# Weight scales from sums of squares on ScalarE, and attention's probabilities turned in nine whole pieces

## What is computed

```
layer 0:  proj = rms_norm(x) @ w_in        -> u, z_a, h, b, c, z_b (512 columns each)
          y_a  = pool_mixer(u) * silu(z_a) # running means over windows 2, 4, 8, 16, less u,
                                           # a 128x128 map for each group, a scale
          y_b  = b * conv3(c * h) * silu(z_b)
          x    = x + concat(y_a, y_b) @ w_out
layer 1:  proj = rms_norm(x) @ w_in        -> query latent (768), key/value latent (256),
                                           # shared rotary key (32), gate (1024)
          q, k, v from the latents: 16 heads, 64 + 32 wide; rms_norm of q and k per head
          p    = softmax(mask(q @ k.T)); o = p @ v  # causal, in blocks of 128 queries
          x    = x + (o * silu(gate)) @ w_out
```

## Time and profile before

| | us |
|---|---|
| median of 3 runs (range) | 961.5 (960.9 to 961.76) |
| the profiled execution, span | 960.9 |
| PE busy | 947.5 (99%) |
| DVE busy | 812.9 (85%) |
| ACT busy | 575.2 (60%) |
| POOL busy | 353.1 (37%) |
| DVE line 2497 (`low`), 192 operations | 102.1, 554 ns each |
| ACT line 2360 (`high`), 192 operations | 89.1 |

### The profile page before, as it was taken

The page is one execution under the profiler, slowest core; times in us unless marked ns, Lnnn a source line. Parts: engine busy times, 40 slices in busy tenths (PEclk is TensorE's granted clock), DMA queues, the critical chain, the costliest instruction groups (busy, mean ns, idle before and its releaser), DMA issues.

```text
span 960.9 us, 17257 instructions
## 1 busy us (share of the span) xinstructions
PE 947.5 (99%) x6406; PEld 671.3 (70%) x6406; DVE 812.9 (85%) x1410; ACT 575.2 (60%) x1076; POOL 353.1 (37%) x393
## 2 busy tenths in 40 slices
PE   9999999999999999999999999998999999999998
PEld 8788544444688887644457999996788888887443
DVE  5798899899865579988887899998999999998763
ACT  6443544424434454454646888866899989997230
POOL 0002233222000002235412577875652478894220
PEclk9999999999999999999999999999999999999999
DMA  9320422111054422332123264566676775460231
GB/s 305 45 61 23 110 77 56 44 45 45 1 175 155 152 67 67 107 112 58 31 72 111 89 205 150 204 181 176 119 163 145 171 150 122 82 179 2 88 110 65
DMA packets 165347, 103.74 MB, mean 108 GB/s; under 512 B 75272, under 2 KB 149520, under 8 KB 165008
## 3 DMA queue, kind: packets, MB, share of 16 engines
q1 hardware_dynamic: 159216, 102.25, 38.0%
q10 hardware_dynamic: 6048, 0.39, 0.5%
HBM read 56.48 MB, written 29.36 MB: 89 GB/s over the span
## 4 chain that ended last, share of the span: by engine, by line
PE 72%; DVE 19%; POOL 3%; issue 3%; ACT 2%; DVEq 0%; POOLq 0%; ACTq 0%
PE banks L111 19%; PE banks L113 19%; PE banks L112 19%; PE banks L2728 7%; PE banks L2746 2%; PE banks L2748 2%; PE banks L2747 2%; DVE heads_y L2480 1%; POOL heads_prod L2616 1%; DVE heads_x L2476 1%; DVE heads_x L2475 1%; DVE front_lt L1223 1%; DVE heads_ss L2522 1%; PE banks L2756 1%; DVE front_l L1223 1%
## 5 line engine op out<-in xcount | busy, mean ns | idle before, releaser
L2497 DVE TENSOR_TENSOR heads_pt_lo<-banks,heads_pt_hi 128x512 f16<-128x512 f32 (+2 forms) x192 | 102.1, 554 | 10.8 <-ACT heads_pt_hi L2360 7.8
L2360 ACT ACTIVATE heads_pt_hi<-banks 128x512 f16<-128x512 f32 (+2 forms) x192 | 89.1, 487 | 9.1 <-PE banks L2728 8.9
L2748 PE MATMUL banks<-heads_v,heads_pt_lo 128*128 128x64 f16 x576 | 71.1, 194 | 0.0
L2747 PE MATMUL banks<-heads_v,heads_pt_hi 128*128 128x64 f16 x576 | 71.0, 194 | 0.0
L2489 DVE CUSTOM_DVE_ANT_0 heads_probs_big<-banks,heads_mask,score_scale 128x1024 f32<-128x1024 f32 (+1 forms) x64 | 68.6, 1072 | 2.9 <-PE banks L113 2.7
L2746 PE MATMUL banks<-heads_v,heads_pt_hi 128*128 128x64 f16 x576 | 70.9, 194 | 0.0
L2728 PE MATMUL banks<-ident,heads_probs_big 128*128 128x128 f32 x416 | 69.5, 281 | 1.2 <-ACT heads_probs_big L2351 1.1
L2351 ACT ACTIVATE heads_probs_big<-heads_probs_big,heads_neg_max 128x1024 f32<-128x1024 f32 (+1 forms) x64 | 63.4, 990 | 8.8 <-DVE heads_neg_max L2489 7.7
L111 PE MATMUL banks<-heads_k_t,heads_q_t 96*128 96x512 f16 (+2 forms) x192 | 63.0, 328 | 1.0 <-DVE heads_neg_max L2489 1.0
L111 PE MATMUL banks<-front_act_hi,front_w_hi 128*128 128x512 f32 x160 | 63.8, 399 | 0.0
L113 PE MATMUL banks<-front_act_hi,front_w_lo 128*128 128x512 f32 x160 | 62.4, 390 | 0.0
(11 more groups left out here) (489 smaller groups left out, 3114.5 us busy)
## 6 DMA issues: line engine op xcount, KB each, us to landing
qk_scratch<-heads_y SPq DMA_DIRECT2D x22, 512.0 KB, 3.7
front_x<-in_x_t SPq DMA_DIRECT2D x16, 512.0 KB, 5.3
front_raw<-in_w_in_ab SPq DMA_DIRECT2D x14, 512.0 KB, 5.1
qk_scratch<-heads_last_y SPq DMA_DIRECT2D x10, 512.0 KB, 3.8
front_w<-in_w_out_ab SPq DMA_DIRECT2D x8, 512.0 KB, 3.9
x_scratch<-front_x SPq DMA_DIRECT2D x8, 512.0 KB, 3.9
v_scratch<-heads_v SPq DMA_DIRECT2D x32, 128.0 KB, 3.0
heads_v_st<-v_scratch SPq DMA_DIRECT2D x8, 512.0 KB, 5.2
```

Of the source, the lines that this page charges most:

```text
L2360: nc.scalar.activation(pt_hi[:, q % PIECES, :width], t_ps[:, banks[("piece", n, k)] % 3, :width], ACT.Copy).then_inc(pt_high, 1)
L2497: nc.vector.tensor_tensor(pt_lo[:, q % PIECES, :width], t_ps[:, banks[("piece", n, k)] % 3, :width], pt_hi[:, q % PIECES, :width], ALU.sub ...
L2747: nc.tensor.matmul(o_part, pt_hi[:, q % PIECES, blk], v2[e][:, j, VH:], start=False, stop=False)
L2748: last = nc.tensor.matmul(o_part, pt_lo[:, q % PIECES, blk], v2[e][:, j, :VH], start=False, stop=(j == i))
```

## The change

1. `pair_peak` and `peak` go. ACT gets `pair_norm`: one ACTIVATE with Square over the same 128x2048 weights, whose accumulated sum per partition takes the place of the maximum. Its elementwise result goes to a scratch tile. It stands behind ACT's snapshot 1 and ahead of `first_tap` and snapshot 2 in pairs 1 to 6; behind snapshot 1 in pairs 8 to 12; other places for pairs 0, 1, 8 and the three of the output.
2. `norm_scale` takes the scale from the sum of squares: one more DVE operation than before.
3. `pair_scale` moves: in `conv` from before the wait for the tap to the end, in `pool_sums` from the middle to the end.
4. PE's `row_sum` moves behind i = 3 in pairs 1 to 12.
5. Attention: another `ORDER`, and nine pieces per head, each a whole 512 columns; three of the nine hold blocks of two tiles. The order of the turns and products within a step, and the access patterns of what comes behind, follow from it. The number of turned blocks and of products stays.

```diff
-ORDER = (7, 3, 6, 2, 5, 1, 4, 0)
+ORDER = (7, 3, 5, 1, 6, 0, 4, 2)
+PIECE_BLOCKS = ([(0, j) for j in range(4)], [(0, j) for j in range(4, 8)], [(1, j) for j in range(4)],
+                [(2, j) for j in range(4)], [(2, 4), (2, 5), (3, 0), (3, 1)],
+                [(4, j) for j in range(4)], [(4, 4), (4, 5), (4, 6), (5, 0)],
+                [(6, j) for j in range(4)], [(6, 4), (7, 0), (7, 1), (7, 2)])
...
+def norm_scale(nc, link, total, size, scale):
+
+    top = float(0x5F3759DF + (13 << 23))
+    link(nc.vector.tensor_scalar(size, total, TINY, None, ALU.max))
+    link(nc.vector.tensor_scalar(scale.bitcast(I32), size.bitcast(I32), -0.5, top, ALU.mult, ALU.add))
+    link(nc.vector.reciprocal(size, scale))
...
+        def pair_norm(p):
+            raw_landed(act, p)
+            if p > 1:
+                act.wait_ge(row_spread, p - 1)
...
+            source = x[:, 0:CHUNKS, BANK:] if p == 0 else raw(p)[:].rearrange("p m (h k) c -> p (m h) (k c)", h=2)
+            nc.scalar.activation(dump[:], source, ACT.Square, accum_out=w_row[:, p % 2:p % 2 + 1]).then_inc(row_peak, 1)
...
                 snapshot(p, 1)
+                if p and p + 1 < PAIRED:
+                    pair_norm(p + 1)
                 if p and p % 2 == 0:
                     first_tap(g - 1)
...
                 snapshot(p, 1)
+                if not last_pair:
+                    pair_norm(p + 1)
...
         high(ROPE0)
+        pair_norm(PAIRED)
         pair_forms(PAIRED, range(FORMS))
...
                 src, n, step = dst, n + 1, 2 * step
-            if p < PAIRED:
-                pair_scale(p)
             link(nc.vector.tensor_scalar(head[:, :win], count[:, :win], float(win), None, ALU.min))
...
             nc.vector.tensor_tensor(d_lo[:], other, f32(d_hi[:]), ALU.subtract).then_inc(d_ready, 1)
+            if p < PAIRED:
+                pair_scale(p)
...
             dve.sem_inc(ch_ready, 1)
-            if p < PAIRED:
-                pair_scale(p)
             dve.wait_ge(tapped, g + 1)
...
             link(nc.vector.tensor_tensor(acc, acc, bb[:], ALU.mult))
             dve.sem_inc(convolved, 1)
+            if p < PAIRED:
+                pair_scale(p)
...
-        def pair_peak(p):
-            raw_landed(dve, p)
-            if p > 1:
-                dve.wait_ge(row_spread, p - 1)
-            nc.vector.tensor_reduce(w_row[:, p % 2:p % 2 + 1], x[:, 0:CHUNKS, BANK:] if p == 0 else
-                                    raw(p)[:].rearrange("p m k c -> p (m k c)"), AX_XY if p == 0 else AX_X, ALU.max,
-                                    apply_absolute_value=True).then_inc(row_peak, 1)
...
-            link(nc.vector.tensor_scalar(w_size[:, one], spread_ps(p), TINY, 2.0 ** -13, ALU.max, ALU.mult))
-            link(nc.vector.reciprocal(w_scale[:, one], w_size[:, one]))
+            norm_scale(nc, link, spread_ps(p), w_size[:, one], w_scale[:, one])
...
                     pair_product(p, i)
-                    if p + 1 < PAIRED and i == (1 if p else 4):
+                    if p + 1 < PAIRED and i == (3 if p else 4):
                         row_sum(p + 1)
...
                     pair_product(p, i)
-                    if p + 1 < ALL_PAIRS and i == 2:
+                    if p + 1 < ALL_PAIRS and i == 3:
                         row_sum(p + 1)
...
+    def pieces_at(n):
 
         h, p = divmod(n, NT)
-        return PER_HEAD * h + sum(len(pieces(ORDER[x])) for x in range(p)) + k
+        return [PER_HEAD * h + x for x, blocks in enumerate(PIECE_BLOCKS) if blocks[-1][0] == p]
...
-            if k == 0:
-                pe.wait_ge(exp_done, n + 1)
-            for r, j in enumerate(pieces(tile_of(n)[1])[k]):
+            pe.wait_ge(exp_done, blocks_of(q)[-1][0] + 1)
+            for r, (n, j) in enumerate(blocks_of(q)):
...
-            for k in range(max(new_pieces, old_pieces)):
-                if k < new_pieces:
-                    transposes(n, k)
-                if k < old_pieces:
-                    product(old, k)
+            for k in range(max(len(new_pieces), len(old_pieces))):
+                if k < len(new_pieces):
+                    transposes(new_pieces[k])
+                if k < len(old_pieces):
+                    product(old_pieces[k])
```

More of the change, by code:

```diff
@@ L2414, in scalar @@
             if n < N:
-                for k in range(len(pieces(tile_of(n)[1]))):
-                    high(n, k)
+                for q in pieces_at(n):
+                    high(q)
             if n + AHEAD < N:
@@ L2437, in scalar @@
         for q in range(1, out.OUT_PAIRS):
+            out.pair_norm(act, q)
             out.forms_high(act, q)
@@ L2543, in vector @@
             if n < N:
-                for k in range(len(pieces(tile_of(n)[1]))):
-                    low(n, k)
+                for q in pieces_at(n):
+                    low(q)
                 if n % 4 == 3:
```

119 lines of the change are left out of this document (61 added, 58 removed).

## The result

The changed kernel takes 971.25 us (median of 4 runs, 970.54 to 972.53) against 961.63 for the kernel before: a ratio of 1.010, 95% interval 1.0087 to 1.0113, so 9.6 us slower. The forecast was 963.7 with a range up to 967.0. The side was right; the size was not.

A forecast was written before the change was run, and what follows sets the result against it. PE was taken as the bound, busy for 947.5 of 960.9 us. Norm and scale +6.6, pair 1 -0.9, pairs 3, 5, 7 +0.3, pairs 8 to 13 -1.4, attention -2.5: +2.1 on 961.5, rounded to 963.7; range 960.2 to 967.0.

The forecast's parts named there:

- norm ahead of the tap, pairs 2, 4, 6: ACT's norm, taken as 1.95 us, makes the tap 1.5, 1.1 and 1.35 us later: +3.95.
- bare scale, the same pairs: At the end of `conv` nothing hides the scale: 0.9 us per pair, +2.7, between 1.5 and 2.7.
- pair 1: `row_sum` moves behind product 3, past the wait for ACT's snapshot, and nothing replaces that wait: -0.88 us.
- pairs 3, 5, 7: Pair 3 stays free of a stall and pair 5 gets 0.3 us worse: +0.3, between -0.4 and +0.7.
- pair 8: DVE reaches the scale earlier, so the stalls of 0.53 and 0.74 us go: -1.27, between 0 and -1.27.
- pair 11 and the rest to 13: Pair 11 gains 0.35 of its 1.19 us; later row sums in pairs 12 and 13 cost +0.2.
- attention, all of it: Fewer switches and smaller stalls at its start and end: -2.5 us, from -0.5 to -4.5.
- switches saved: In attention, one turn per head instead of four stands right behind a product: -1.5 us.
- end: At attention's end, spread short tiles and joined pieces leave 0.1 of a 0.61 us stall: -0.5.
- rival 2: The clock falls behind the front's new waits, one to three stretches of 1.7 us: 965.4 to 968.8; chance 0.12.
- rival 5: POOL's sums block DVE's doublings in pairs 3 and 5, 1.6 us on top: 965.2; chance 0.08.
- signs of being wrong: Tap not late; three stalls growing under 3 or over 9 us; attention's 690 to 865 changing by over 4.5 us.

The follow-up runs named there:

- scales_only: Parts 1 to 4 of the change alone on the kernel before, with attention as before: 969.08 us, ratio 1.0077.
- reduction_back: The changed kernel with DVE's reduction over the weights put back in pairs 1 to 6 and 8 to 12, its result unused: 973.94 us, ratio 1.0126.

## Why the prediction was right or wrong

The number failed in attention above all, where -2.5 was forecast and +2.6 came. The terms, by the starts of PE's matmuls in the profiled executions:

| step | forecast | measured |
|---|---|---|
| norm ahead of the tap, pairs 2, 4, 6 | +3.95 | +3.7 |
| bare scale, the same pairs | +2.7 | +2.2 |
| clock behind those waits | a rival, 0.12 | +1.7 |
| pair 1 | -0.88 | +0.34 |
| pairs 3, 5, 7 | +0.3 | +0.15 |
| pair 8 | -1.27 | -1.28 |
| pair 11 and the rest to 13 | -0.15 | +0.7 |
| attention, all of it | -2.5 | +2.6 |
| of this: switches saved | -1.5 | -1.1 |
| of this: start, up to the fourth head | -0.5 | -0.4 |
| of this: waits ahead of turns | 0 | +3.0 |
| of this: end | -0.5 | +0.6 |
| the output | 0 | 0 |

The four parts of attention come to 2.1; some 0.5 of the 2.6 is not assigned.

**The tap and the scale** were right as a mechanism and nearly in size, pair by pair: the norm took 1.89 for the 1.95 of the sum. The scale is less than 0.9 a pair because a pause of 0.5 in front of `conv_out` took up part of it; the prediction had this as its lower bound, 1.5.

**The clock** was rival 2, at 0.12. It named the place, the length of the waits, 1.7 us a stretch, and 965.4 to 968.8 for it. What spoke against it, that the waits lie 38 us apart, did not hold: in each of the three profiles with waits of 2.3 us and more (the changed kernel, `scales_only`, `reduction_back`) just one of them is followed by 3 us at 0.50 to 0.56 of the clock, in pair 2, 6 and 4, and in none with waits of 1.2 or less. Which wait it follows changed from kernel to kernel, and by the clocks on record two of the changed kernel's four executions most likely have no such stretch, while all four of `scales_only` do. What decides it is not shown.

**Pair 1** failed at "nothing replaces it". I looked at PE's next need of the row sum and not at PE's next wait of any kind. `front_cb` was already just in time, behind a PE that was itself held by the row sum; moving the row sum alone gave 0.0 of the 0.88. The earlier start of the sums gave nothing either: POOL's sums took back some 2.25 us, and the scale at the end of the chain with the wait for ACT's form behind it 1.6. The first is rival 5, the doublings held up by POOL, which was priced for pairs 3 and 5; it came in pair 1, and for pair 11's tables, where DVE was done 0.5 us later behind the start of the pair (13.06 against 12.59) than before, without its 2.28 us of reduction. In pairs 3 and 5, where it was looked for, it cost 0.15.

**Pair 8** was right to the tenth. **Pair 11** was the wrong sign, by the same contention, and by a wait of 0.32 behind the row sum. The row sum itself is on time there; the product after it waits for ACT's last snapshot, and ACT has no pause from the norm to that snapshot:

```profile
465.88 1.90 ACT L754 ACTIVATE front_norm_dump<-front_raw_even 128x2048 f16<-128x2048 f32 x1
...
468.96 1.06 ACT L878 ACTIVATE front_squares<-latent 128x1024 f32<-128x1024 f32 x1
469.92 0.67 ACT L760 ACTIVATE front_later_snap<-banks,front_unscale 128x512 f32<-128x512 f32 x1
```

**Attention** is the largest error, 5.1 us, and its step is the sentence that the fewer operations on DVE are "worth nothing" since PE has no idle time from 690 to 865. That was half of the argument: with PE at 175.00 of 175, nothing can be gained, but something can be lost. I averaged DVE's and ACT's room over a stretch and took it for slack. The slack that counted was per tile, 0.26 us between tile 6's exponentials and its turns, 0.12 of it free, and the distance could be read from the trace before. The edit moved tile 6 behind short tiles, and gave DVE whole pieces, for which it waits longer (22.4 us against 10.8). The saved switches were real, 1.1 us of the 1.5. The end of attention went the wrong way as well: 0.5 was to be gained because the new order spreads the short tiles, and the stall grew from 0.62 to 0.93 and 0.26. "Blocks that wait are turned one step later at most, under the two steps of lead" counted the lead in steps, and the steps are not equally long. Of the signs of being wrong that the prediction named none came: the tap was late, the three stalls grew by 5.9, within 3 to 9, and attention changed by 2.6, under 4.5. But what the last one was to show, a chain over DVE and not PE setting the pace in attention, is what the runs showed; its threshold was set too wide.

The sum of the front without the clock would have been 5.6 for a forecast of 4.6. Of the error of 7.7 us in the profiled execution, 1.0 is this, 1.7 the clock and 5.1 attention.

## What to carry to other kernels

Where an engine shows no idle time, its feeders' slack has to be read per hand-over (the end of what it waits for against the start of its work), not from their busy share: a busy PE can hide that each of its inputs is just in time, and such a place can only lose. A wait that is removed is worth what the next one leaves: look for the next before counting it. And a long operation placed in an engine's idle gap ahead of work that waits anyway was free here, while the same operation ahead of a step on the path cost its length less the idle time in front of it, and what came with it.

## What the runs showed of the hardware that was not expected

- VectorE beside GpSimd's TENSOR_TENSOR: operations on 128x2 took 0.93 to 1.12 us in place of 0.16, and a cast of 128x1024 with one input 1.73 in place of 0.69. A TENSOR_REDUCE of 128x2048 took 2.28 beside the same work.
- TensorE's clock: behind waits of 2.3 to 2.7 us with steady work on both sides, a stretch of about 3 us at 1.2 GHz behind one of three such waits, in each of three profiles; it cost 1.7 us. Behind waits up to 1.2 us in the front there was none. Of the changed kernel's four executions most likely two had it.
- ScalarE's Square over 128x2048 with its sum: 1.90 us, 0.19 for the read of the accumulator, 1.89 until the next operation starts. A snapshot of 0.69 lets the next one start after 0.59, so the read adds about 0.1 (an estimate from these rows).
